# Two mixture-of-experts layers in a fused two-block network: context products behind two quarters of latents, router logits on column tiles, latents ranked first

## What is computed

```python
def expert_choice_ffn(h, w_router, w1, w3, w2):
    B, T, D = h.shape                       # D = 1024, 16 experts, D_FF_EXPERT = 1024
    cap = max(1, EC_CAPACITY * T // N_EXPERTS)   # 64 of 512 latents, 32 of 256 context tokens
    aff = jax.nn.softmax((h @ w_router).astype(jnp.float32), axis=-1)
    gate, idx = lax.top_k(jnp.swapaxes(aff, 1, 2), cap)
    xin = jax.vmap(lambda hb, ib: hb[ib])(h, idx)
    hid = jax.nn.silu(jnp.einsum('becd,edf->becf', xin, w1)) * jnp.einsum('becd,edf->becf', xin, w3)
    y = jnp.einsum('becf,efd->becd', hid, w2) * gate[..., None].astype(h.dtype)
    return jax.vmap(lambda yb, ib: jax.ops.segment_sum(
        yb.reshape(-1, D), ib.reshape(-1), num_segments=T))(y, idx)
```

## Time and profile before

| | us |
|---|---|
| median of 3 runs (lowest to highest) | 4749.61 (4744.96 to 4751.13) |
| the profiled execution, its own time | 4743.4 |
| its span in the profile | 4741.7 |
| TensorE busy in the span | 4076.9 (86%) |
| VectorE / ScalarE / GpSimd busy | 1667.3 / 1132.2 / 419.6 |

### The profile page before, as it was taken

How to read it: one execution, slowest core, us unless ns; L and a number is a source line. 1 busy time by engine, 2 the same in 40 slices (tenths; PEclk the granted TensorE clock), 3 DMA queues, 4 the chain that set the end, 5 groups by cost and what they waited for, 6 DMA issues and landing times. The chain is left out here.

```text
span 4741.7 us, 58914 instructions
## 1 busy us (share of the span) xinstructions
PE 4076.9 (86%) x25735; PEld 2268.6 (48%) x25735; DVE 1667.3 (35%) x2916; ACT 1132.2 (24%) x2162; POOL 419.6 (9%) x428
## 2 busy tenths in 40 slices
PE   7988879999998985548998578887988998988998
PEld 4546644222223433437898352223456754446763
DVE  2215421122124116845543422223554322454321
ACT  2114311111103126723343010001133212123211
POOL 2200020000000012300000200000001200001200
PEclk9999988999999996766797789999989998999999
DMA  6231124988973217753332349998112222112220
GB/s 223 107 140 40 48 103 171 323 281 281 324 267 137 79 42 271 249 149 86 91 93 73 147 190 409 409 409 343 38 36 89 98 80 73 57 36 89 98 80 36
DMA packets 360625, 746.44 MB, mean 157 GB/s; under 512 B 67344, under 2 KB 143616, under 8 KB 360368
## 3 DMA queue, kind: packets, MB, share of 16 engines
q1 hardware_dynamic: 348960, 700.55, 41.6%
q0 software_dynamic: 11408, 42.13, 2.5%
HBM read 680.73 MB, written 61.89 MB: 157 GB/s over the span
## 5 line engine op out<-in xcount | busy, mean ns | idle before, releaser
L62 PE MATMUL ps<-raw,xinT 128*64 128x512 f32 (+1 forms) x4096 | 653.4, 503 | 58.4 <-DMA raw<-in_moe_w_dram 50.6
L62 PE MATMUL ps<-c,hT 128*128 128x512 f32 (+2 forms) x1024 | 420.0, 565 | 5.4 <-ACT hT L72 3.1
L62 PEld LDWEIGHTS ps<-raw,xinT 128*64 128x64 f32 (+1 forms) x4096 | 157.3, 122 | 542.8 <-issue 407.5
L62 PE MATMUL ps<-wp,hp 128*128 128x512 f32 x1536 | 360.2, 396 | 20.4 <-DVE wp L75 20.4
L62 PE MATMUL ps<-a,nahT 128*128 128x512 f32 x768 | 338.2, 597 | 5.6 <-ACT nahT L72 5.2
L62 PEld LDWEIGHTS ps<-wp,hp 128*128 128x128 f32 x1536 | 290.7, 189 | 87.2 <-issue 27.5
L62 PEld LDWEIGHTS ps<-c,hT 128*128 128x128 f32 x1024 | 192.2, 192 | 200.1 <-issue 192.2
L62 PE MATMUL ps<-raw,hidT 128*64 128x512 f32 x1024 | 260.3, 610 | 19.7 <-DMA raw<-in_moe_w_dram 19.2
L62 PEld LDWEIGHTS ps<-a,nahT 128*128 128x128 f32 x768 | 144.1, 191 | 178.7 <-issue 178.0
L62 PE MATMUL ps<-c,oT 128*128 128x512 f32 x512 | 222.8, 592 | 1.4 <-ACT oT L72 1.4
L62 PEld LDWEIGHTS ps<-c,oT 128*128 128x128 f32 x512 | 97.0, 190 | 117.0 <-issue 111.0
(11 more groups left out here) (449 smaller groups left out, 5958.1 us busy)
## 6 DMA issues: line engine op xcount, KB each, us to landing
raw<-in_moe_w_dram SPq DMA_DIRECT2D x384, 1024.0 KB, 14.3
c<-in_w_in_dram SPq DMA_DIRECT2D x28, 2048.0 KB, 8.9
a<-in_ada_w_dram SPq DMA_DIRECT2D x16, 2048.0 KB, 12.9
b<-in_ada_w_dram SPq DMA_DIRECT2D x8, 2048.0 KB, 10.0
a<-in_na_w_qkv_dram SPq DMA_DIRECT2D x6, 2048.0 KB, 19.1
c<-in_w_branch_dram SPq DMA_DIRECT2D x16, 512.0 KB, 4.2
c<-in_w_out_dram SPq DMA_DIRECT2D x4, 2048.0 KB, 8.9
c<-in_w_ple_gate_dram SPq DMA_DIRECT2D x4, 2048.0 KB, 7.9
```

The source lines that it names most:

```text
L62: return self.e.matmul(out, lhsT, rhs, start=start, stop=stop, skip_group_check=True) if self.e is not None else self
```

## The change

- **Order of the products in moe0.** The plan's `quarter` becomes `latents` and `tokens`. In moe0 two quarters of latents (8 matmuls on tiles of 64) are followed by the same two quarters of context (16 matmuls on tiles of 32); both quarters are signalled free in the context's pass. In moe1 nothing of that changes.
- **Logits.** The router is now the stationary operand, padded to 32 columns with zeros, and the 512 (256) transposed tokens move; blocks k and k + 4 use column tile k. ScalarE copies the four partial sums (`lg`), and one small matmul a chunk against `fold`, four stacked identities, adds them up.
- **Ranking.** The latents are ranked, masked, scanned, turned and gathered (both halves) first; the context's ranking comes behind on VectorE and its gather last. The copy to `work` and the subtraction of 1 go (the slots are numbered from 1). `sel` has four more buffers, so the second half's one-hots don't wait.
- **Slot weights** are gathered on one column tile, and VectorE copies them to both halves of the partitions.
- **ScalarE** makes the exponential ahead of the `tokhigh` copies. GpSimd clears `wr` and builds `fold`; SyncE's router load waits for the clearing.
- **Ends.** `P.end(k_('experts'), P.pe)` stands ahead of the last group's scatter. The rounding and the residue of `Y` go by halves, and `Y` no longer waits for `Ycw`. `rwx` is allocated behind the smaller tiles.

```diff
...
-    wr = P.sb([128, 8, 16], name="wr", ctx=d)
-    sel = P.sb([128, nch, 512], F32R, name="sel", ctx=d)
+    fold = P.sb([128, 16], name="fold", ctx=d)
+    sel = P.sb([128, nch + 4, 512], F32R, name="sel", ctx=d)
...
-    mask = P.sb([16, T], name="mask", ctx=d)
-    ones = P.sb([16, T], name="mones", ctx=d)
+    one = P.sb([16, 1], name="mone", ctx=d)
...
+    lg = xinT[:].rearrange("p k e m -> p (k e m)")[:, 8 * T + D:9 * T + D]
+    wr = xinT[:].rearrange("p k e m -> p (k e m)")[:, 9 * T + D:9 * T + D + 256].rearrange("p (k e) -> p k e", k=8)
...
-    groups = [(0, chunks[0], 0, 8, 64)] + ([(1, chunks[1], 0, 16, 32)] if two else []) + [(0, chunks[0], 8, 8, 64)]
+    spans = [slice(ch[0] * 128, ch[-1] * 128 + 128) for ch in chunks]
+    groups = [(0, chunks[0], 0, 8, 64), (0, chunks[0], 8, 8, 64)] + ([(1, chunks[1], 0, 16, 32)] if two else [])
+    sel_of = lambda gi, i: sel[:, nch + i if gi == 1 else i, :]
...
+        for s, sp_ in enumerate(spans):
+            rb, rfree = P.banks.take(k_('parts', s), (P.act, name, 'parts', s))
...
+            for k in range(8):
+                j = k % 4
+                e.wait_ge(*(P.act.at(name, 'hC', k // 2) if s else (P.act if k % 2 else P.dve).at(name, 'hT', k)))
+                ins = e.matmul(P.psum[32 * j:32 * j + 32, rb, 0:sp_.stop - sp_.start], wr[:, k, :], hT[:, k, sp_], k < 4, k >= 4)
+            ins.then_inc(*P.pe.inc(name, 'parts', s))
...
-        for k in range(8):
-            e.wait_ge(*(P.act if k % 2 else P.dve).at(name, 'hT', k))
-            if two:
-                e.wait_ge(*P.act.at(name, 'hC', k // 2))
-            for ch in range(nch):
-                ins = e.matmul(P.psum[:, rb, ch * 16:ch * 16 + 16], hT[:, k, ch * 128:(ch + 1) * 128], wr[:, k, :], (k, ch) == (0, 0), k == 7)
+        for ch in range(nch):
+            e.wait_ge(*P.act.at(name, 'parts', ch // 4))
+            ins = e.matmul(P.psum[:, rb, ch * 16:ch * 16 + 16], lg[:, ch * 128:(ch + 1) * 128], fold[:], ch == 0, True)
...
+        def places(ch):
+            for i in ch:
+                e.wait_ge(*P.dve.at(name, 'posn', ch[0]))
...
+                e.turn(P.psum[:, b, 0:16], posn[:, i * 128:(i + 1) * 128], P.ident).then_inc(*P.pe.inc(name, 'posT', i))
...
+        places(chunks[0])
...
                     for i in ch:
-                        for h in range(2):
-                            ins = e.matmul(P.psum[64 * h:64 * h + 64, wb, e0 + ex:e0 + ex + 1], sel[:, i, ex * cp:(ex + 1) * cp].bitcast(F32),
-                                           aff[:, i, e0 + ex:e0 + ex + 1], i == ch[0], i == ch[-1])
+                        ins = e.matmul(P.psum[0:64, wb, e0 + ex:e0 + ex + 1], sel_of(gi, i)[:, ex * cp:(ex + 1) * cp].bitcast(F32),
+                                       aff[:, i, e0 + ex:e0 + ex + 1], i == ch[0], i == ch[-1])
                 ins.then_inc(*P.pe.inc(name, 'wslot', gi))
+            if two and gi == 0:
+                places(chunks[1])
...
+        for s, sp_ in enumerate(spans):
+            e.wait_ge(*P.pe.at(name, 'parts', s))
+            e.activation(lg[:, sp_], P.bank(name, 'parts', s)[:, 0:sp_.stop - sp_.start], ACT.Copy).then_inc(*P.act.inc(name, 'parts', s))
+        e.wait_ge(*P.dve.at(name, 'centred'))
+        e.activation(aff[:], aff[:], ACT.Exp).then_inc(*P.act.inc(name, 'exp'))
         for ch in range(nch):
             e.wait_ge(*P.dve.at(name, 'normed', ch))
             e.activation(hl[:, 0, ch], x[:, ch], ACT.Copy).then_inc(*P.act.inc(name, 'tokhigh', ch))
-        e.wait_ge(*P.dve.at(name, 'centred'))
-        e.activation(aff[:], aff[:], ACT.Exp).then_inc(*P.act.inc(name, 'exp'))
...
-        e.wait_ge(*P.dve.last())
-        e.tensor_copy(work[:], affT).then_inc(*P.dve.inc())
...
+        def ranked(s):
+
+            v, frm = work[:, spans[s]], affT[:, spans[s]]
...
-                e.max(m8[:], v).then_inc(*P.dve.inc())
+                e.max(m8[:], frm).then_inc(*P.dve.inc())
...
-                e.match_replace(v, m8[:], v, -1.0).then_inc(*P.dve.inc())
-        e.wait_ge(*P.dve.last())
-        e.tensor_scalar(mask[:], work[:], -1.0, None, ALU.is_equal).then_inc(*P.dve.inc())
...
-            e.tensor_tensor_scan(posn[:, v], ones[:, v], mask[:, v], 0.0, MUL, ADD).then_inc(*P.dve.inc())
...
-        e.tensor_tensor(posn, posn, mask[:], MUL).then_inc(*P.dve.inc())
-        e.wait_ge(*P.dve.last())
-        e.tensor_scalar(posn, posn, -1.0, None, ADD).then_inc(*P.dve.inc(name, 'posn'))
...
+                e.match_replace(v, m8[:], frm, -1.0).then_inc(*P.dve.inc())
+                frm = v
...
+            e.tensor_scalar(v, v, -1.0, None, ALU.is_equal).then_inc(*P.dve.inc())
...
+            e.tensor_tensor_scan(posn[:, spans[s]], one[:].to_broadcast([16, len(chunks[s]) * 128]), v, 0.0, MUL, ADD).then_inc(*P.dve.inc())
...
+            e.tensor_tensor(posn[:, spans[s]], posn[:, spans[s]], v, MUL).then_inc(*P.dve.inc(name, 'posn', chunks[s][0]))
...
-            if gi == len(groups) - 1:
-                e.wait_ge(*P.pe.at(name, 'wslot', 0))
+            if gi != 1:
+                ranked(s)
...
-                e.tensor_tensor(sel[:, i, :].rearrange("p (e s) -> p e s", e=ne),
+                e.tensor_tensor(sel_of(gi, i).rearrange("p (e s) -> p e s", e=ne),
...
-        e.wait_ge(*P.pe.at(name, 'wslot', len(groups) - 1))
-        e.tensor_copy(wslot[:], P.bank(name, 'wslot')[:, 0:16]).then_inc(*P.dve.inc(name, 'wslot'))
+        e.wait_ge(*P.pe.at(name, 'wslot', 1))
+        for h in range(2):
+            e.tensor_copy(wslot[64 * h:64 * h + 64, :], P.bank(name, 'wslot')[0:64, 0:16]).then_inc(*P.dve.inc())
+        P.dve.name(name, 'wslot')
...
+        e.memset(one[:], 1.0).then_inc(*P.pool.inc(name, 'one'))
+        e.memset(wr, 0.0).then_inc(*P.pool.inc(name, 'wr'))
+        for j in range(3):
+            e.wait_ge(*P.pool.at('identity'))
+            e.wait_ge(*P.pool.last())
+            e.tensor_tensor(fold[:], fold[:] if j else P.ident[:, 0:16], P.ident[:, 32 * j + 32:32 * j + 48], ADD).then_inc(*P.pool.inc())
+        P.pool.name(name, 'fold')
...
-        e.dma_start(wr[:], I['moe_router'][l].rearrange("(k p) e -> p k e", p=128)).then_inc(*s_wr.inc(name))
+        e.wait_ge(*P.pool.at(name, 'wr'))
+        e.dma_start(wr[:, :, 0:16], I['moe_router'][l].rearrange("(k p) e -> p k e", p=128)).then_inc(*s_wr.inc(name))
...
-        for q in range(4):
-            plan.append(('quarter', next(quarters), q, p))
+
+        for q in range(0, 4, 2 if nch == 6 else 1):
+            plan.append(('latents', q, p))
             tick()
+            if nch == 6:
+                plan.append(('tokens', q, p))
+                tick()
...
+            if what == 'latents':
+                q, p = a
...
-                e.wait_ge(*H.loaded(u))
-                W = H.raw[:, u % H.nr]
-                for k in range(2):
-                    kk = 2 * q + k
-                    for t in range(2):
+                for i in range(2 if two else 1):
+                    e.wait_ge(*H.loaded(done + i))
+                    W = H.raw[:, (done + i) % H.nr]
+                    for k in range(2):
+                        kk = 2 * (q + i) + k
                         X = xinT[:, kk, ex, 0:64] if kind == 'A' else hidT[:, ex % 2, kk]
-                        ins = e.matmul(P.psum[half(t), bank[0], :], X, W[:, k, cols(t if kind == 'A' else swap(t, ex))], kk == 0, kk == 7)
-                    for j in range(4 if two else 0):
+                        for t in range(2):
+                            ins = e.matmul(P.psum[half(t), bank[0], :], X, W[:, k, cols(t if kind == 'A' else swap(t, ex))], kk == 0, kk == 7)
+                if not two:
+                    ins.then_inc(*P.pe.inc(name, 'quarter', done))
+                    done += 1
+                    if q == 3:
+                        P.pe.name(name, 'product', *p)
+            elif what == 'tokens':
+                q, p = a
+                kind, ex, w = p
+                for i in range(2):
+                    W = H.raw[:, done % H.nr]
+                    for k in range(2):
+                        kk = 2 * (q + i) + k
                         X = xinT[:, kk, ex, 64:96] if kind == 'A' else hicT[:, ex % 2, kk]
-                        ins = e.matmul(P.psum[part(j), bank[1], 0:256], X, W[:, k, blk(j)], kk == 0, kk == 7)
-                ins.then_inc(*P.pe.inc(name, 'quarter', u))
-                if q == 3:
+                        for j in range(4):
+                            ins = e.matmul(P.psum[part(j), bank[1], 0:256], X, W[:, k, blk(j)], kk == 0, kk == 7)
+                    ins.then_inc(*P.pe.inc(name, 'quarter', done))
+                    done += 1
...
+                if (g, i) == (len(GROUPS) - 1, 0):
+                    P.end(k_('experts'), P.pe)
...
-        P.end(k_('experts'), P.pe)
...
-                P.act.name(name, 'keep', ex)
+                    e.activation(Y[half(t), pair(ex), swap(t, ex), 0, :], Yw[half(t)], ACT.Copy).then_inc(*P.act.inc(name, 'keep', ex, t))
...
```

(15 more changed lines are left out.)

47 lines of the change are left out of this document (20 added, 27 removed).

## The result

| | before | after |
|---|---|---|
| median of 4 runs each, us | 4748.69 | 4636.08 |
| lowest to highest | 4744.96 to 4751.13 | 4633.39 to 4639.33 |
| profiled execution, its own time | 4743.4 | 4639.33 |

The ratio is 0.9764, 95% interval 0.9747 to 0.9781: 112.6 us less, where 109.7 had been summed.

The account below looks back on a forecast made before the run. TensorE was taken to bound moe0's products, the weights' DMA moe1's, chains the routing. Terms -79 + 9.3 - 17.7 - 9.7 - 5.1 - 7.5 = -109.7 us gave 4640 us; main case 4622 to 4660, 8-in-10 range 4622 to 4682.

Parts of the forecast that it names:

- Part 1, the products: moe0's expert products: grouping latents and context by two quarters saves tile-width changes of 0.28 us there and back, -79 us.
- Rival (a): moe0's products: only half of the tile cost goes, 42 us, giving 4675 us; chance 0.14.
- Rival (b): moe0 becomes bound by DMA, 46 us of the gain gone, giving 4686 us; chance 0.06.
- The ring: Start of moe0's products: one wait for quarter 7's late refill, +7.4 us, plus low clock +2.4, sum +9.3 us.
- the fourth pair could start at 16.5 and needs quarter 7: moe0's products: that pair waits from 16.5 us until quarter 7 lands at 23.9, costing +7.4 us once.
- Rival (c): moe0's weight buffers starve; a landing of 15.3 us costs 137 us, giving 4777 us; chance 0.02.
- The banks and the openings: moe0's products: four openings for other work per product and the order of taking banks stay the same; no cost.
- I set these against each other: moe0: third gather now starts cold behind small matmuls, first product warm; taken to cancel, no net time.
- Routing: Stages ahead of the experts: tiled logits, reordered ranking and fewer waits, -17.7 us in moe0 and -9.7 in moe1.
- up to 2.3: moe0's routing: VectorE's mask and scan could meet GpSimd's subtractions and lose at most 2.3 us.
- Ends: Last scatters and next stages' starts: residue by halves and an earlier fence, -5.1 us in moe0, -7.5 in moe1.
- (d): A later stage absorbs the shift, the two ends' 12 us fall away, 4652 us; no separate chance given.

Follow-up runs that it names:

- experiment 1: Changed kernel with moe0's products alone put back to latents then context for every block, buffers refilled singly: 4715.6 us, +79.5.
- experiment 2: Changed kernel with one quarter of latents, then its context, in moe0's products: 4656.0 us, +19.9.
- experiment 7: Changed kernel with both the later residual load and the gate's banks held longer in moe0: 4620.1 us, -16.0.
- experiment 4: Changed kernel with the latents of all four quarters of a product ahead of its context: 4657.2 us, +21.1.
- Experiment 6: Changed kernel with the two banks of product (A, ex, 0) released behind the first two quarters of (A, ex, 1): 4632.5 us, -3.6.
- experiment 3: Kernel before with only the new order of moe0's products, routing and ends as before: 4673.8 us beside 4752.0, -78.1.
- experiment 11: Changed kernel with one expert's slot weights gathered behind each eighth of a gather, not all eight behind the whole: 4642.3 us, +6.2.
- experiment 9: Changed kernel with the router's logits as before, one 16-column matmul per block and chunk, no copy or fold: 4647.1 us, +11.0.
- experiment 10: Changed kernel with slot weights gathered on two column tiles again, twice as many instructions: 4637.5 us in one run.
- Experiment 8: Changed kernel with TensorE's point for the next stage's fence back behind the last scatters in both layers: 4646.9 us, +10.8.
- experiment 5: Changed kernel with SyncE issuing moe0's 3 MB of residual 23 refills later: 4628.6 us, -7.4.
- experiment 12: Changed kernel with later residual, held banks and slot weights between the eighths of a gather together: 4630.0 us.

## Why the prediction was right, and where its terms were off

**Part 1, the products.** The mechanism and its size were right: 0.28 us there and back was worked out from the rows of three timelines, 0.29 measured from 192 and 96 changes. 288 fewer changes are 83.1 us of TensorE's busy time, where 79 stood. Rival (a), half of the cost, had been given 0.14 because the rows could not split a start from a change; experiment 1 gives back 76.2 us where (a) foresaw 42, and experiment 2 shows the same price for every change. Rival (b), the DMA as the bound, is refuted by 376 GB/s with TensorE busy throughout and by experiment 7.

**The ring.** Right in kind, 2 us too dear. The step "the fourth pair could start at 16.5 and needs quarter 7" took a pair as one wait; the code waits for each quarter, so quarter 6 ran first and the wait was 5.88 us. Quarter 7 was there 24.2 us into the products, where 23.9 stood. The clock behind it cost 2.1 where 2.4 stood. Rival (c) was placed right: experiment 4 shows it begin one step beyond this change, and at 0.2 to 1.15 us a wait it costs the gain of the saved changes, not the 137 us that its formula with a landing of 15.3 us gave.

**The banks and the openings.** The sentence that they stay the same held: four waits on `hic` of 6.97 us before, four of 6.96 after, and four in each experiment that leaves the rotation alone. Experiment 6 shows what these waits come from, product (A, ex, 1) coming round to the banks that gate (ex, 0) is still reading, and that 7 us can be had there. It was tried in the changed kernel only.

**Cold starts.** "I set these against each other" was right to within a microsecond: the first product warm gives 2.8 us back (experiment 3), the additional cold gather costs 1.6 to 1.8 (experiment 11) and the first gather 0.5. Setting them against each other hid that they fall in different rows of the table above: +2.4 in the gathers where +0.6 was summed, and more than that saved in the products. Together: -83.1 + 5.4 (wait on `raw`, less the 0.49 of before) + 2.1 - 2.8 = -78.4 for the products, measured -78.1.

**Routing.** -18.1 where -18.3 stood, -7.0 where -6.6, -3.1 where -3.1. The logits are 12.3 and 4.5 us of it (experiment 9), predicted 12.1 and 4.4. GpSimd beside VectorE did show in moe0: the mask took 0.76 us where the same one in moe1 took 0.41, the product 1.02 where 0.68. That is 0.7 us, inside the "up to 2.3". GpSimd's timeline there:

```profile
688.56 13.87 POOL L75 TENSOR_TENSOR hl<-mx,hl 128x1024 fp32r<-128x1024 f32 x6 [13.69 <-ACT hl L72]
...
703.32 1.16 POOL L111 TENSOR_SCALAR_AFFINE_SELECT bcc<-bcc 16x512 f32<-16x512 f32 x1
```

The mask (701.95 to 702.71) ended 0.28 us behind the last subtraction, the product (703.99 to 705.01) 0.53 behind the select, which itself took 1.16 us where it took 0.72 in the kernel before. By the rule of the Trainium skill, "SBUF — State Buffer", section "SBUF: two separate sides", a VectorE instruction with two inputs in SBUF and a GpSimd instruction that reads SBUF exclude each other for a whole instruction. The product, which has two, agrees with it. The mask has one; the same section also names a VectorE instruction in a 2-port mode, which no row here shows. The slot weights came at nothing, as taken, and experiment 10 gives the reason.

**Ends.** -5.3 and -7.3 where -5.1 and -7.5 stood, closer than the spread of these stretches allows to say. Experiment 8 confirms that the fence's point carries most of each, and refutes (d).

The sum was 109.7, the changed stretches gave 116.5 in the trace and 112.6 in the medians. The 6.8 us between the sum and the trace are known, to half a microsecond: 4.1 us too little for the changes of width, 1.8 too much for the ring, and 2.8 for the warm first product, less the 1.8 by which the gathers of moe0 came out dearer. That the median lies within 3 us of the sum is in part luck: with the unchanged stretches in it, the profiled pair alone gives 104.1.

## What to carry to other kernels

When TensorE alternates between tiles of different widths, count the changes: 0.29 us for each there and back, so group the passes, but only as far as the ring's buffers allow, since the buffers held are the price. Before you charge a wait to a change, list the same wait in the kernel before; the four on the bank rotation stood in both kernels alike. They also show where to look next: where a rotation comes round to a bank that is just being read. Keep every large load out of the first refills of a ring. Before spreading small matmuls to keep the clock up, add up what each change of width costs.

## What the runs showed of the hardware that was not expected

- A change of tile width costs the same whether the runs of 64-column matmuls between are 1.0 or 3.6 us long: 0.288 us there and back from 192 changes, 0.290 from 96 (experiments 1, 2 and 7). Between 128 and 64 columns some 0.26 us, if the remainder in experiment 11 is that.
- One-column matmuls on two column tiles run side by side: 128 passes on two tiles took 3.90 us (experiment 10), 64 on one took 3.89.
- A pause of 5.9 us left TensorE at half clock (0.50) for some 4 us, until 788.8 us, which cost 2.1 us (experiment 5). moe0's first gather ran cold for one eighth in experiment 11 (3.51 us) and for two in experiment 12 (3.78 each), with the same instructions ahead of it.
- MAX and MATCH_REPLACE over 512 columns took 0.68 and 0.66 us both beside GpSimd's subtractions and without them, while the mask that met the last subtraction grew by 0.35 us, and the product that met GpSimd's select by 0.34.
